# VectorE's output copies and its subtraction trade places in both attentions of a two-layer backbone

## The reference

```python
def attend(q, k, v, mask=None, sink=None):
    s = jnp.einsum('bqhgd,bkhd->bhgqk', q, k).astype(jnp.float32) * (HEAD_DIM ** -0.5)
    ...
    m = jnp.max(s, axis=-1, keepdims=True)
    ...
    e = jnp.exp(s - m)
    den = jnp.sum(e, axis=-1, keepdims=True)
    if sink is not None:
        den = den + jnp.exp(sk - m)
    p = (e / den).astype(v.dtype)
    return jnp.einsum('bhgqk,bkhd->bqhgd', p, v)
```

## Time and profile before

| | |
|---|---|
| device time, median of 3 runs (range) | 1680.92 us (1678.32 to 1681.75) |
| the profiled execution: its own time, its span | 1683.92 us, 1682.1 us |
| TensorE busy with matmuls | 1528.1 us, 91% of the span |
| VectorE, ScalarE, GpSimd busy | 972.9, 723.8 and 616.6 us |
| attention of layer 0, attention of layer 1 | up to 317.8 us of the span; up to 1273.1 us of the span |

### The profile page before, as it was taken

One profiled execution on the slowest core, in us unless ns is written; L12 is line 12 of the kernel. 1 busy time (PEld: TensorE's weight loads), 2 busy tenths in 40 slices (PEclk: granted clock), 3 DMA queues, 4 the chain that ended last, 5 costly groups with the idle time before them and its releaser, 6 DMA issues.

```text
span 1682.1 us, 22280 instructions
## 1 busy us (share of the span) xinstructions
PE 1528.1 (91%) x7584; PEld 1221.8 (73%) x7584; DVE 972.9 (58%) x1457; ACT 723.8 (43%) x1234; POOL 616.6 (37%) x537
## 2 busy tenths in 40 slices
PE   6988788889999999999999687789988899999998
PEld 1777456677888888887888466567776688887886
DVE  2457577458668766633344656578775544444355
ACT  3432466534323333223353633277773544443453
POOL 1351344242222222222333625264541444443444
PEclk9999899899999999999999898899999899999999
DMA  9130850104355434401112212010001233332222
GB/s 337 34 94 1 281 170 2 50 15 140 117 155 175 128 106 129 123 32 51 65 63 70 63 38 63 14 50 1 1 1 51 73 91 99 100 96 67 80 95 100
DMA packets 129136, 143.86 MB, mean 86 GB/s; under 512 B 7160, under 2 KB 95484, under 8 KB 129064
## 3 DMA queue, kind: packets, MB, share of 16 engines
q1 hardware_dynamic: 129064, 142.91, 26.9%
HBM read 140.79 MB, written 2.10 MB: 85 GB/s over the span
## 4 chain that ended last, share of the span: by engine, by line
PE 76%; DVE 10%; ACT 5%; POOL 4%; issue 3%; DMA 2%; SPq 0%; POOLq 0%; DVEq 0%; ACTq 0%
PE ps L461 21%; PE ps L462 21%; PE ps L463 21%; PE ps L1349 3%; PE ps L1335 2%; PE ps L1360 2%; DVE hT_lo L780 2%; ACT pT_hi L1400 1%; DVE hT_hi L778 1%; ACT prob L1389 1%; PE ps L1362 1%; DMA start_w<-in_ada_w_dram 1%; DVE o_tmp L1459 1%; PE ps L665 1%; POOL w_lo L453 1%
## 5 line engine op out<-in xcount | busy, mean ns | idle before, releaser
L453 POOL TENSOR_TENSOR w_lo<-raw,w_hi 128x1024 fp32r<-128x1024 f32 (+1 forms) x192 | 368.5, 1921 | 650.4 <-ACT w_hi L446 650.4
L461 PE MATMUL ps<-hT_hi,w_hi 128*128 128x512 f32 (+1 forms) x1072 | 383.3, 358 | 5.9 <-DVE hT_lo L780 5.0
L462 PE MATMUL ps<-hT_lo,w_hi 128*128 128x512 f32 (+1 forms) x1072 | 380.9, 355 | 0.0
L463 PE MATMUL ps<-hT_hi,w_lo 128*128 128x512 f32 (+1 forms) x1072 | 378.4, 353 | 0.0
L446 ACT ACTIVATE w_hi<-raw 128x1024 fp32r<-128x1024 f32 (+1 forms) x200 | 172.6, 865 | 183.5 <-PE ps L463 161.2
L461 PEld LDWEIGHTS ps<-hT_hi,w_hi 128*128 128x128 f32 x1072 | 202.5, 189 | 45.4 <-DVE hT_lo L780 8.6
L463 PEld LDWEIGHTS ps<-hT_hi,w_lo 128*128 128x128 f32 x1072 | 201.8, 188 | 29.8
L462 PEld LDWEIGHTS ps<-hT_lo,w_hi 128*128 128x128 f32 x1072 | 202.5, 189 | 27.7
L1961 DVE TENSOR_TENSOR g_lo<-act_g,g_hi 128x768 fp32r<-128x768 f32 (+1 forms) x84 | 106.7, 1277 | 165.5 <-ACT g_hi L1911 164.2
L461 PE MATMUL ps<-w_hi,g_hi 128*128 128x512 f32 x420 | 166.3, 396 | 3.5 <-DVE g_lo L1961 3.0
L463 PE MATMUL ps<-w_hi,g_lo 128*128 128x512 f32 x420 | 163.7, 390 | 0.0
(11 more groups left out here) (230 smaller groups left out, 2512.4 us busy)
## 6 DMA issues: line engine op xcount, KB each, us to landing
raw<-in_ffn_w_up_dram SPq DMA_DIRECT2D x84, 512.0 KB, 3.9
ada_w_up<-in_ada_w_dram SPq DMA_DIRECT2D x48, 512.0 KB, 4.1
raw<-in_ffn_w_down_dram SPq DMA_DIRECT2D x84, 256.0 KB, 2.6
ada_w<-in_ada_w_dram SPq DMA_DIRECT2D x32, 512.0 KB, 5.2
start_w<-in_ada_w_dram SPq DMA_DIRECT2D x8, 1024.0 KB, 10.8
raw<-in_c_w_qkv_dram SPq DMA_DIRECT2D x12, 512.0 KB, 3.6
raw<-in_ab_w_in_dram SPq DMA_DIRECT2D x8, 512.0 KB, 4.0
raw<-in_ab_w_out_dram SPq DMA_DIRECT2D x8, 512.0 KB, 3.8
```

Of the source, the lines that this page charges most:

```text
L453: by.tensor_tensor(w_lo[:, slot, 0:width], raw[:, n % RAW, 0:width], w_hi[:, slot, 0:width].bitcast(F32), ALU.subtract).then_inc(lo_split, 1)
L461: nc.tensor.matmul(outp, s_hi, m_hi, start=first, stop=False, skip_group_check=True)
L462: nc.tensor.matmul(outp, s_hi, m_lo, start=False, stop=False, skip_group_check=True)
L463: return nc.tensor.matmul(outp, s_lo, m_hi, start=False, stop=last, skip_group_check=True)
```

## The change

A new function goes through the list of steps before VectorE walks it. Where it finds a `T`, any step, and an `O` in a row, it takes the `O` to the front of the three. The other engines walk the list as before. It applies to 11 of the 12 groups of layer 0 and to 15 of the 16 of layer 1; the last group of each phase has no `T` ahead of its `O`. No instruction is added or removed; VectorE's two copies (L1459) now stand ahead of one subtraction (L1451) instead of behind it.

```diff
+        def outputs_first(steps):
+
+            out = list(steps)
+            for n in range(len(out) - 2):
+                if out[n][0] == "T" and out[n + 2][0] == "O":
+                    out[n:n + 3] = [out[n + 2], out[n], out[n + 1]]
+            return out
+
         def attn_vector(dve, l, before):
             groups, steps, first = attn_setup(l)
+            steps = outputs_first(steps)
             after_phase(dve, before)
             nden = 2 if l == 0 else 1
```

## The result

| | before | changed |
|---|---|---|
| device time, median of 7 runs each (range) | 1679.55 us (1678.32 to 1682.48) | 1668.52 us (1665.72 to 1673.93) |
| the profiled execution, its span | 1683.92, 1682.1 us | 1667.24, 1665.4 us |
| granted clock of the profiled execution | 0.966 | 0.971 |

The changed kernel takes 0.9933 of the time, 95% interval 0.9918 to 0.9948: 11.3 us less by the ratio, between 8.7 and 13.8. The forecast was 8.4 us. The measured time stands at the very lower edge of the range (1668.5) and outside the forecast's own (1670.9 to 1674.8). The direction and the mechanism in the open handovers hold. The size is off by about a third, and that is two errors of mechanism and a piece of TensorE's clock, partly against each other; the last part takes them one by one.

The account below looks back on a forecast made before the run. TensorE was taken to bound the kernel, busy 91% of the span, with 14.2 us of waits for VectorE's copies reachable. Layer 1's 4.3 plus layer 0's 4.1 gave 8.4 us: 1680.92 to 1672.5 us, range 1668.5 to 1678.0.

Parts of the forecast that it names:

- What is late next: At handovers, ScalarE's copies become last releaser; bubble of 0.67 us closes, later transposes come earlier, 0.58 us gained per handover.
- the sign of being wrong: Layer 0's small VectorE instruction L1420: its time going up by more than 3 us in all would refute the forecast.
- Rival 1: Later subtraction or another engine bounds most groups; 0.25 us per handover, 4.0 us saved, 1676.9 us; chance 0.20.
- rival 2: Products `V` come earlier, then wait for the exponential or GpSimd in all groups; end unmoved, 1680.9 us; chance 0.08.
- Groups 0 and 1 of layer 1: ScalarE's weight split of 1.06 us behind its copies holds the transposes; gain 0.1 us each, bounds 0 and 0.3.
- Six groups have no such wait, since an output-projection fill covers it; they gain nothing: Layer 1: six groups where a fill covers the wait for VectorE's copies; gain 0.
- TensorE is free at 1.82 - 0.67 = +1.15: Group 2 of layer 1: TensorE free 1.15 us after the last `V`, so the 0.67 us bubble closes almost entirely.
- I cost it at nothing: Layer 0: GpSimd's earlier work delaying VectorE's small instruction by 0.2 us, paid for by 0.18 gained; 0 per handover.
- rival 3: Layer 0: GpSimd holds VectorE, 0.58 us in each of 11 handovers, up to 2.04 with a split; slower, chance 0.06.
- the gain is the shift of the copies: Layer 0's three waits of 1.38 us and more: gain at most 0.68 each, 1.7 us together.
- Windows 7 to 10: Layer 0: group 7 gains 0.2 us, groups 8 and 9 0.4 each through GpSimd, group 10 0.7.
- rival 4: Less idling near layer 0's group 10 keeps TensorE's clock up; 4 of 5.2 us comes back, 1668.5 us; chance 0.04.

Follow-up runs that it names:

- the extra wait: Changed kernel with each group's first product also waiting for the moved subtraction; 0.9959 of the kernel before, 6.9 us less.
- the one-tensor instructions: Layer 0's two small VectorE instructions written with one tensor and a per-partition scalar operand; against before, 0.9879 in the changed kernel, 0.9974 in the old order.
- the moved splits: Changed kernel with layer 1's four weight splits one place later in the list; ratio 0.9991 against the kernel before.
- the last pair: On one chip: kernel before with layer 0's two small VectorE instructions rewritten, 0.9974 of before; and the changed kernel again, 0.9920.

## Where the prediction was right and where it was wrong

**The place and the mechanism: right.** TensorE waited for a bank whose readers stood behind an unhurried subtraction. With the extra wait put back, three quarters of layer 1's gain goes.

**What is late next: right.** ScalarE's copies became the last releaser. The transposes of chunk 3 came 0.58 earlier in the example, and the six windows shortened by 0.55 to 0.59. The new wait for the subtraction doesn't show: L1349 waits for it 0.8 us in three places in layer 1, before and after. GpSimd's addition starts 0.59 to 0.63 earlier at every handover, and L1420's time grew by 0.5 us, where I had put 3 as the sign of being wrong. Rival 1, half of it comes back, is out, and so is rival 2.

**Groups 0 and 1 of layer 1: right in size.** They gained 0.06 (forecast 0.1).

**"Six groups have no such wait, since an output-projection fill covers it; they gain nothing": wrong.** They gained 0.20 to 0.23 each, 1.3 us in all, and the experiment with those six alone gives 1.2. The same step had capped the first three windows of layer 0 at their idle column: forecast 0.7 in all, measured 1.4 (0.47, 0.45, 0.48). The failed step is the reading of TensorE's idle time as its whole standstill: "TensorE is free at 1.82 - 0.67 = +1.15" is the end of a record, and the product started at +1.09. The idle time is short by the 0.24 us by which following products overlap. It could have been read in the kernel before from nearly any such pair of rows without a wait: the product starts 0.35 us after the first of four transposes whose record lasts 0.60. This step put 2.0 us too little into the sum.

**Windows 3, 4 and 5 of layer 0: wrong, too high.** Forecast 1.7 us together; measured 0.51, -0.16 and 0.25, 0.6 in all. The price that I had put at nothing ("I cost it at nothing") was real here. GpSimd's split of the sums, 0.6 us earlier, got ahead of VectorE's next small instruction and held it for 0.5 us. This is rival 3's mechanism, in its mild form. Taking the hold away shortened the windows 4 and 5 by 0.3 each. That is not the whole shortfall of window 4, which then gains 0.2 on the old order where 0.58 was forecast. The second thing that failed there is "the gain is the shift of the copies". VectorE's own queue (copies, subtraction, a gate step and the small instructions) is full: with the one-tensor instructions it never idles for more than 0.07 us at a time behind group 4, from +0.2 to +4.2, in either order. There the next product starts at +1.32 in the new order and at +1.91 in the old one, but VectorE's subtraction of the next chunk starts at +3.09 against +2.95, and the one behind it at +3.70 against +3.72. A swap inside a full queue doesn't bring forward what stands behind it. That is read from the rows; no experiment took work out of this queue.

**Windows 7 to 10: about right, apart from the clock.** Windows 8 and 9 gave 0.58 each, forecast 0.4. To take the clock out I compare with the old order's windows where TensorE was at the higher level, 9.62 and 3.77 in the kernel with only layer 1's covered windows changed: window 7 gave 0.14 and window 10 gave 0.74, forecast 0.2 and 0.7.

| | forecast | measured, clock taken out |
|---|---|---|
| layer 1: six open windows | 3.5 | 3.4 |
| layer 1: six covered windows | 0 | 1.3 |
| layer 1: groups 0, 1 and 14 | 0.85 | 0.7 |
| layer 0: windows 0 to 2 | 0.7 | 1.4 |
| layer 0: windows 3 to 5 | 1.7 | 0.6 |
| layer 0: windows 7 to 10 | 1.7 | 2.0 |
| sum | 8.4 | 9.4 |

**The clock.** The attentions explain 9.4 of the 11.3 us. That is 1.0 over the forecast: 2.0 too little for TensorE's idle time against 1.1 too much for the windows 3 to 5, and small differences. The remaining 1.9 us had no term in the sum: rival 4 had the clock at 4 us, at the end of layer 0's attention, with a chance of 0.04. That the whole time came out so near the clock case (1668.5) is luck, since 2.0 us of it are the idle time's and not the clock's.

At rival 4's own place it is right in kind and too large. The wait of 2.60 us shrank to 1.88, and the products behind it ran at the higher level. About 0.9 us came back there (4.64 against 3.77 with the old order in either state). With the new order on VectorE window 10 of layer 0 was free of the lower level in all six profiles, with the old order in two of five. In window 7 the clock came and went with either order.

More lies where nothing was changed. From layer 1's last `V` to the end the kernel before took 411.3 us in its profile and the changed kernel 407.4. Matched product by product, 1.3 us of the 3.9 are lost right behind the attention, where TensorE was at the lower level from 1272.6 to 1279.4 us in the one and for half as long in the other, and 2.4 us at one place later on. This is the place, first in the kernel before and then in the changed one; the granted clock is the number behind the busy times:

```profile
1552.00:1559.00 7.00, 4.96 (x8) 2.64 (x9) 3.56 (x6) 2.59 (x5) 1.19 (x1) 0.53 0.11 37
```

```profile
1537.90:1544.90 7.00, 5.05 (x19) 3.56 (x20) 3.47 (x6) 2.82 (x6) 1.10 (x1) 1.00 0.13 37
```

Over all twelve profiles this part takes 407.4 to 407.5 us four times, each with the whole of layer 1 in the new order, and 408.6 to 411.3 us eight times, of which one has that order (with the moved splits), one has it with the extra wait and one has it on ScalarE too. The means over the executions point the same way: on the chip of the last pair the clock was 0.970 over the changed kernel's and 0.967 over those of the kernel before. So the rest of the gain is seen to be the clock's in the profiles; whether the new order brings it about was not tested.

## What to carry to other kernels

Swap two steps in an engine's queue when the one behind has its inputs first and somebody idle waits for its result; the copies and the rounding show both signs of it, a gain of 0.58 us on VectorE and a loss of all of it on ScalarE. When sizing a wait of TensorE, compare start to start with a place where the same pair follows without a wait, since the idle column leaves out the overlap of its records. And look at what a step that comes earlier starts on other engines: GpSimd's work, moved ahead, took back 0.3 us in each of two windows, and two rewritten instructions gave that back and removed an old hold of 2.2 us too. Where the engine's queue is full, a swap inside it helps only the step that it moves forward.

## What the runs showed of the hardware

A small VectorE instruction with two tensors from SBUF stood for up to 2.38 us while GpSimd worked, and with one tensor and a scalar operand per partition it took 0.20 to 0.22 us in all 96 cases, 36 of which ran beside a GpSimd instruction. It costs 0.05 us more when nothing is in its way (0.16 with two tensors). VectorE and ScalarE read the two halves of one PSUM bank at the same time over 0.7 us at all handovers but group 10's in layer 0 (before, for under 0.2 us), with no change in the copies' duration: 0.407 to 0.420 us each on VectorE against 0.405 to 0.419 before.
